# A fused streaming-encoder trunk on one core: the first pair of retention heads in halves of the features, its loads reordered, and two units of the conditioning vector made on TensorE

## The chip, the cores and the metric

The kernel runs on one core of a Trainium2 chip. The metric is the device time of one execution in microseconds (us), as the median of several runs. TensorE does the matmuls, VectorE (DVE in the rows) and ScalarE (ACT) the element-wise work, GpSimd (POOL) the rotary embedding and masks, and the SyncE queue (SP) issues nearly all transfers from HBM.

## The reference

The trunk has two layers. Each layer modulates a normed input with a conditioning vector, mixes over tokens, and then applies a channel mixer. The first mixer is retention with 8 heads, the second a stick-breaking attention; the first channel mixer is a dense SwiGLU, the second a top-2-of-8 expert SwiGLU. The input is 256 tokens of 1024 features, all in float32. What bears on this change is the beginning of the first layer:

```python
cond = jax.nn.silu(c)                                  # 1024 numbers
mod = cond @ ada_w[i] + ada_b[i]                       # ada_w[i]: 1024 x 6144
sh_m, sc_m, g_m, sh_f, sc_f, g_f = jnp.split(mod, 6, axis=-1)
h = modulate(rms_norm(x, norm_mix[i]), sh_m, sc_m)     # h * (1 + scale) + shift
y = retention(h, ...)                                  # starts with proj = h @ w_in, 1024 x 6144
q, k = rope(q), rope(k)
x = x + g_m[:, None, :] * y
```

## The kernel before

**Weights.** Every weight is fetched in chunks of 1 MB (a tile of 512 columns has two chunks, one for features 0 to 511 and one for 512 to 1023) into a ring of six raw buffers. ScalarE rounds a chunk into `w_hi` (L1079, two instructions of 128x1024), VectorE subtracts to get `w_lo` (L1449, two instructions), in a ring of three. TensorE then makes each product in three passes, `hi*hi`, `hi*lo`, `lo*hi` (L500, L501, L502, function `passes`). In the first layer the 256 tokens are two blocks, so a chunk is 24 matmuls of 128x512. Chunks 0 and 1 are queries and keys of the first two heads, 2 and 3 their values, 4 and 5 their gates; chunks 6 to 11 are those of the second pair of heads, and so on.

**The conditioning vector.** `cond @ ada_w` is made in units of 512 columns. For a unit VectorE adds eight slices of the weights, each times one column of `cond`, into `acc` (`ada_steps`: one L1465, seven L1468). TensorE transposes `acc` with four matmuls (`reduce_ada`, L539), and VectorE adds up the result and the bias (`mod_out`, L1487 and L1489). A unit's weights are two loads of 1 MB into the two halves of `ada` (`load_ada`, L285); each half is issued when the same half of the unit before has been read. Units 0 and 1 are the shift of the first layer, unit 2 the first half of its scale. The second half of the scale is not made so but with columns of `cond` as the moving operand: 32 float32 matmuls (64 passes, L573) from a tile of weights that is put into raw buffers 4 and 5 (`ada_first`).

**The start, in the order of each engine.**

- SP: unit 0, `x`, positions and frequencies, `ada_first`, unit 1, chunk 0, unit 2, chunks 1, 2, 3; then a wait until the columns have been read, and chunks 4 and 5.
- TensorE: transposes of unit 0, of the normed `x` (`transpose_x`, L546, eight matmuls per block of tokens), the 64 passes of the columns, transposes of units 1 and 2; then chunks 0 and 1 by blocks of tokens.
- VectorE: unit 0, the rotary angles (L1543 to L1559), the two normed blocks (L1500), units 1 and 2, `scol` (1 + scale times the gain of the norm), and per block `modulate` (L1510) and the split of `hT_lo` (L1515). ScalarE does the other half of the features (L1111) and `hT_hi` (L1118).

**The first pair and the loop.** Per pair of heads TensorE multiplies the tile of queries and keys, then that of values, waits for the rotary embedding (`roped`, six GpSimd instructions L463 to L470, which start when ScalarE has copied the queries and keys out with L1161), transposes them (L659), multiplies the gates, and makes the scores (L672, L673). The scores are masked on VectorE (`decayed`, L1596) and multiplied with the values (`mix`, L631 to L633) after the next pair's queries and keys. VectorE weaves the splits of weights with the steps of two units per pair (`woven`); the first pair makes units 3 and 4. The remaining three pairs are one loop, whose PE order is:

```python
pe.wait_ge(qk_ev, i)
pe.wait_ge(mod_ok, 2 * i + 1)
tile(0, m, (0, 1))
pe.wait_ge(mod_ok, 2 * i + 2)
mix(i - 1)
pe.wait_ge(qk_ev, i + 1)
reduce_ada(4, 0, m - 1)
```

Semaphores order all of this; nothing is planned at run time. An engine works in the order of its own program, so an instruction that waits holds up all behind it.

Of the kernel before, what the change touches and what calls it, by code (L numbers as in the profile page):

```python
# [16 lines left out]
P = 128  # L17
# [34 lines left out]
def trunk(nc, x_d, c_d, pos_d, ada_w, ada_b, norm_mix, norm_ff, ret_w_in, ret_gn, ret_w_out, kv_ada_w,  # L52
# [7 lines left out]
    with ctx:  # L60
# [68 lines left out]
        ada_first = raw[:, 4:6, :]  # L129
# [67 lines left out]
        small_in = sem("small_in"); pos_in = sem("pos_in"); x_in = sem("x_in"); rw_in = sem("rw_in")  # L197
# [6 lines left out]
        ada_step = sem("ada_step"); first_done = sem("first_done"); first_ok = sem("first_ok"); first_in = sem("first_in")  # L204
# [40 lines left out]
        def _(sp):  # L245
# [33 lines left out]
            def load_ada(u, h, k=0):  # L279

                t = u if u < 3 else u + 1
                w, t0 = (ada_w[0], 0) if t < 12 else (kv_ada_w, 12) if t < 16 else (ada_w[1], 16)
                if u > 0:
                    sp.wait_ge(ada_step, 8 * (u - 1) + 4 * (h + 1) + 16 * k)
                sp.dma_start(ada[:, h, :].rearrange("p (t n) -> p t n", t=4),  # L285
                             cols_of(w, h * 4 * P, k * 2 * TW + (t - t0) * TW, TW)).then_inc(ada_in[h], 16)


            for row, src in ((0, ada_b[0]), (48, kv_ada_b), (64, ada_b[1])):
                n = src.shape[0] // P  # L290
                sp.dma_start(rows[row:row + n, 0, :], src.rearrange("(r c) -> r c", c=P)).then_inc(small_in, 16)
            load_ada(0, 0)
            load_ada(0, 1)
            sp.dma_start(x[:, :, :], x_d[0].rearrange("(b p) d -> p b d", p=P)).then_inc(x_in, 16)
# [10 lines left out]
            for h in range(2):  # L305
                sp.dma_start(ada_first[:, h, :].rearrange("p (t n) -> p t n", t=4),
                             cols_of(ada_w[0], h * 4 * P, 3 * TW, TW)).then_inc(first_in, 16)
            load_ada(1, 0)
            load_ada(1, 1)
            load_half2(0, 0, w_r, 0, 0, K0)  # L310
            load_ada(2, 0)
            load_ada(2, 1)
            load_half2(1, 0, w_r, 4 * P, 0, K0)
            load_tile(2, 0, w_r, 0, V0)
            sp.wait_ge(first_done, 1)
            load_tile(4, 0, w_r, 0, G0)
            with sp.Fori(0, PAIRS - 1) as k:
                load_half2(6, k, w_r, 0, k * 2 * DK + 2 * DK, k * 2 * DK + (2 * DK + K0))
                load_ada(3, 0, k)
                load_half2(7, k, w_r, 4 * P, k * 2 * DK + 2 * DK, k * 2 * DK + (2 * DK + K0))  # L320
                load_ada(3, 1, k)
# [5 lines left out]
                load_ada(4, 0, k)  # L327
                load_half(10, k, w_r, 0, k * 2 * DV + (G0 + 2 * DV))
                load_ada(4, 1, k)
                load_half(11, k, w_r, 4 * P, k * 2 * DV + (G0 + 2 * DV))  # L330

            for m in range(8):
# [4 lines left out]
                if m in (0, 1):  # L337
                    load_ada(9, m)
                if m in (3, 4):
                    load_ada(10, m - 3)  # L340
                if m >= 6:
                    load_ada(11, m - 6)
# [7 lines left out]
            load_ada(12, 0)  # L350
            load_in(c + 2, 0, 1, 0)
            load_ada(12, 1)
            load_in(c + 3, 0, 1, 1)
            load_rows(c + 4, 0, ff_w_out[0], 0)
            load_ada(13, 0)
            load_in(c + 5, 0, 2, 0)
            load_ada(13, 1)
# [3 lines left out]
            load_ada(14, 0)  # L361
            load_in(c + 9, 0, 3, 1)
            load_ada(14, 1)
            load_rows(c + 10, 0, ff_w_out[0], 4 * P)
            with sp.Fori(0, 3) as k:
                for o in range(2):
                    load_in(c + 11 + 3 * o, k, 2 * k + (4 + o), 0)
                    load_in(c + 12 + 3 * o, k, 2 * k + (4 + o), 1)
                    load_ada(15 + o, 0, k)
                    load_rows(c + 13 + 3 * o, k, ff_w_out[0], k * 4 * P + (3 + o) * 2 * P)  # L370
                    load_ada(15 + o, 1, k)
            load_in(c + 29, 0, 10, 0)
            load_in(c + 30, 0, 10, 1)
            load_ada(21, 0)
            load_rows(c + 31, 0, ff_w_out[0], 9 * 2 * P)
            load_ada(21, 1)
# [6 lines left out]
            ada_after = {0: (22, 0), 1: (22, 1), 3: (23, 0), 4: (23, 1), 6: (24, 0), 8: (24, 1), 10: (25, 0), 11: (25, 1),  # L383
                         13: (26, 0), 14: (26, 1)}
# [47 lines left out]
        def _(pool):  # L432
# [47 lines left out]
            diagonal(0, diag0, MIX0 + G, 5)  # L480
            diagonal(1, diag1, FF0 + G, 11)
# [3 lines left out]
            for c in range(KC):  # L485
# [3 lines left out]
                if c == 5:  # L489
                    pool.wait_ge(ada_step, 27 * 8)  # L490
                    diagonal(2, diag2, MIX1 + G, 21)
            pool.wait_ge(gbc_done, 3)
            diagonal(3, diag3, FF1 + G, 27)
# [3 lines left out]
        def _(pe):  # L497
# [44 lines left out]
            def transpose_x(n, b):  # L542

                pe.wait_ge(xn_ok, NB * n + b + 1)
                for c in range(KC):
                    last = pe.transpose(ps[:, 2 * b + c // 4, (c % 4) * P:(c % 4 + 1) * P],  # L546
                                        (xn0 if n == 0 else xn)[:, b, c * P:(c + 1) * P], ident[:, :])
# [16 lines left out]
            reduce_ada(0, 6)  # L564
            transpose_x(0, 0)
            transpose_x(0, 1)

            pe.wait_ge(cond_ok, 1)
            pe.wait_ge(first_in, 32)
            for c in range(4):  # L570
                for kc in range(KC):
                    cols = slice(kc % 4 * TW + c * P, kc % 4 * TW + (c + 1) * P)
                    last = pe.matmul(ps[:, 5, c:c + 1], ada_first[:, kc // 4, cols], cond[:, kc:kc + 1],  # L573
                                     start=kc == 0, stop=kc == KC - 1)
            last.then_inc(first_done, 1)
            reduce_ada(1, 7)
            pe.wait_ge(mod_ok, 1)
            reduce_ada(2, 6)

# [39 lines left out]
            def tile_by_blocks(c, banks, q):  # L619

                for b, bank in enumerate(banks):
                    for h in range(2):
                        block_half(c, h, b, bank, q)
# [12 lines left out]
            def pair_of_heads(i, m):  # L636

                later = not isinstance(i, int)
                if later:
                    pe.wait_ge(qk_ev, i)  # L640
                    pe.wait_ge(mod_ok, 2 * i + 1)
                if later:
                    tile(0, m, (0, 1))
                else:
                    tile_by_blocks(0, (0, 1), 0)
                if later:
                    pe.wait_ge(mod_ok, 2 * i + 2)
                    mix(i - 1)
                    pe.wait_ge(qk_ev, i + 1)
                    reduce_ada(4, 0, m - 1)  # L650
                    pe.wait_ge(gs_ok, i)
                tile(2, m, (2, 3))
                if later:
                    transpose_r(i - 1)
# [10 lines left out]
                reduce_ada(3, 4, m)  # L665
                if later:
                    pe.wait_ge(r32_ok, i)
                else:
                    pe.wait_ge(mod_ok, 3)

                for hd in range(2):
                    pe.matmul(ps[:, 6 + hd, 0:S], qkT[:, 2 + hd, 0:P], qkT[:, hd, :], start=True, stop=True)  # L672
                    last = pe.matmul(ps[:, 6 + hd, S:384], qkT[:, 2 + hd, P:S], qkT[:, hd, P:S], start=True, stop=True)  # L673
                last.then_inc(sc_done, 1)

            pair_of_heads(0, 0)
# [6 lines left out]
            for m in range(5):  # L683
# [3 lines left out]
                if m == 1:  # L687
                    pe.wait_ge(mod_ok, 2 * PAIRS + 2)
                    mix(PAIRS - 1)
                    reduce_ada(10, 6)  # L690
                if m == 3:
                    pe.wait_ge(mod_ok, 11)
# [7 lines left out]
            reduce_ada(11, 4)  # L700
# [4 lines left out]
            reduce_ada(12, 5)  # L705
# [32 lines left out]
            def ff_two(i, m):  # L738

                for o in range(2):  # L740
                    c = U_FF + 2 + 3 * o
                    ff_in(c, m, 2 * i + (1 + o))
                    pe.wait_ge(mod_ok, 2 * i + (13 + o))
                    reduce_ada(13 + o, 3, i)
# [9 lines left out]
            pe.wait_ge(mod_ok, 23)  # L754
            reduce_ada(23, 3)
# [3 lines left out]
            pe.wait_ge(mod_ok, 24)  # L759
# [51 lines left out]
            def reduce_last(u):  # L811

                pe.wait_ge(ada_step, 8 * (u + 1))
                bank = (2, 2, 3)[u - 24]
# [4 lines left out]
            def scores(c):  # L819

                pe.wait_ge(kq_ev, 2 + 2 * (c // 4))
                if c == 1:
                    pe.wait_ge(mod_ok, 25)
# [48 lines left out]
            reduce_last(24)  # L872
# [46 lines left out]
            pe.wait_ge(gbc_ev, 3)  # L919
            reduce_last(25)  # L920
            reduce_last(26)
# [145 lines left out]
        def _(act):  # L1067
# [36 lines left out]
            def modulate(q, n, b, shift, hT_free, dst=hT_hi):  # L1104

                act.wait_ge(xT_done, 4 * n + 2 * b + 1)
                act.wait_ge(scol_ok, q + 1)
# [6 lines left out]
                for i in range(2):  # L1114
                    act.wait_ge(h32b_ok if i else h32a_ok, NB * q + b + 1)
# [19 lines left out]
            act.wait_ge(x_in, 16)  # L1135
            root_table()
            for b in range(NB):
                root_mean_square(0, b)
            act.wait_ge(ang_ok, 1)
            act.activation(sin[:, :, :], red, ACT.Sin).then_inc(rt_ok, 1)  # L1140
            act.activation(cos[:, :, :], tmp_r, ACT.Sin).then_inc(rt_ok, 1)
            split(0)
            split(1)
            split(2)
# [908 lines left out]
```

## Time and profile before

| | |
|---|---|
| median of 3 runs | 1625.49 us (1624.29 to 1627.39) |
| the profiled execution | 1626.12 us, of which the span of the core is 1624.4 us |
| TensorE busy with matmuls | 1549.2 us, 95% of the span |
| VectorE, ScalarE, GpSimd busy | 88%, 67%, 4% of the span |
| moved from and to HBM | 500.91 MB, mean 308 GB/s |
| mean granted clock of TensorE | 0.979 |

Times in the rows are us from the start of the span, unless ns is said. "Busy" of TensorE counts overlapping matmuls once, and a matmul's own duration is longer than the distance to the next one, since they are pipelined. "PEclk" is the share of TensorE's full clock that was granted: 1.00 is 2.4 GHz and 0.50 is 1.2 GHz.

### The profile page before, as it was taken

What the parts mean: (1) busy time and instruction counts of PE and PEld (TensorE: products, weight loads), DVE (VectorE), ACT (ScalarE), POOL (GpSimd) and SP (SyncE); (2) the same over time, 40 slices, a digit from 0 to 9 for tenths busy, and PEclk for the clock granted to TensorE, in tenths of its full rate; (3) what the DMA queues carried; (4) which work ended last, traced back from release to release, by engine and by line L of the source; (5) the groups of instructions that cost most, each with busy time, mean ns of one, the idle gap of its engine ahead of it and who ended that gap; (6) DMA issues with size and microseconds to landing.
All of it is one profiled execution on the core that took longest, in us unless ns stands there. A gap on an engine that the chain in (4) does not pass through costs nothing.

```text
span 1624.4 us, 22887 instructions
## 1 busy us (share of the span) xinstructions
PE 1549.2 (95%) x7310; PEld 1285.2 (79%) x7310; DVE 1422.0 (88%) x1604; ACT 1085.6 (67%) x1224; POOL 58.9 (4%) x47
## 2 busy tenths in 40 slices
PE   4899998999989998999999999999999999999996
PEld 4788876888869776888888888888888888888884
DVE  6989999788878766989989989989989989989995
ACT  3544445344366646878878878878878778778773
POOL 0212200000000110000000000000000000000000
PEclk8899999999999998999999999999999999999998
DMA  9977777788855424999999999999999999999991
GB/s 329 340 259 268 268 262 248 273 299 296 324 187 207 156 79 146 390 370 346 361 379 339 367 373 338 374 375 332 368 377 333 365 380 335 366 381 334 363 380 69
DMA packets 235114, 500.91 MB, mean 308 GB/s; under 512 B 9744, under 2 KB 40640, under 8 KB 235072
## 3 DMA queue, kind: packets, MB, share of 16 engines
q1 hardware_dynamic: 233904, 500.29, 84.8%
q8 instruction: 25, 0.41, 0.1%
q10 hardware_dynamic: 1168, 0.07, 0.1%
q14 instruction: 17, 0.14, 0.0%
HBM read 499.28 MB, written 1.05 MB: 308 GB/s over the span
## 4 chain that ended last, share of the span: by engine, by line
PE 81%; DVE 9%; DMA 4%; issue 3%; ACT 2%; POOL 1%; SPq 0%; DVEq 0%; ACTq 0%; POOLq 0%
PE ps L500 24%; PE ps L502 24%; PE ps L501 24%; DVE acc L1468 3%; DMA ada<-in_ada_w 2%; DVE w_lo L1449 2%; PE ps L981 2%; PE ps L772 1%; PE ps L774 1%; PE ps L776 1%; DMA raw<-in_ret_w_in 1%; DMA ada<-in_kv_ada_w 1%; PE ps L990 1%; PE ps L1014 1%; PE ps L991 0%
## 5 line engine op out<-in xcount | busy, mean ns | idle before, releaser
L1449 DVE TENSOR_TENSOR w_lo<-raw,w_hi 128x1024 fp32r<-128x1024 f32 x834 | 991.0, 1228 | 68.8 <-ACT w_hi L1079 56.6
L1079 ACT ACTIVATE w_hi<-raw 128x1024 fp32r<-128x1024 f32 x834 | 861.3, 1057 | 215.5 <-PE ps L502 189.1
L500 PE MATMUL ps<-w_hi,RA 128*128 128x512 f32 x1528 | 606.4, 397 | 11.4 <-DVE RA L1909 3.7
L502 PE MATMUL ps<-w_hi,RA 128*128 128x512 f32 x1528 | 597.1, 391 | 0.0
L501 PE MATMUL ps<-w_lo,RA 128*128 128x512 f32 x1528 | 596.5, 390 | 0.0
L500 PEld LDWEIGHTS ps<-w_hi,RA 128*128 128x128 f32 x1528 | 287.8, 188 | 70.8 <-issue 4.6
L502 PEld LDWEIGHTS ps<-w_hi,RA 128*128 128x128 f32 x1528 | 287.6, 188 | 61.2
L501 PEld LDWEIGHTS ps<-w_lo,RA 128*128 128x128 f32 x1528 | 288.1, 189 | 58.1 <-issue 0.7
L500 PE MATMUL ps<-w_hi,hT_hi 128*128 128x512 f32 x400 | 161.7, 404 | 10.2 <-DVE hT_lo L1515 6.2
L501 PE MATMUL ps<-w_lo,hT_hi 128*128 128x512 f32 x400 | 158.2, 395 | 0.0
L502 PE MATMUL ps<-w_hi,hT_lo 128*128 128x512 f32 x400 | 158.1, 395 | 0.0
L1468 DVE SCALAR_TENSOR_TENSOR acc<-ada,cond,acc 128x512 f32<-128x512 f32 x189 | 151.6, 802 | 3.1
L500 PEld LDWEIGHTS ps<-w_hi,hT_hi 128*128 128x128 f32 x400 | 76.8, 192 | 26.9 <-DVE hT_lo L1515 7.1
L502 PEld LDWEIGHTS ps<-w_hi,hT_lo 128*128 128x128 f32 x400 | 76.6, 191 | 16.8
L501 PEld LDWEIGHTS ps<-w_lo,hT_hi 128*128 128x128 f32 x400 | 76.9, 192 | 15.3
L1364 ACT ACTIVATE RA<-ps 128x512 fp32r<-128x512 f32 x56 | 33.4, 597 | 56.4 <-PE ps L981 56.4
L1898 DVE TENSOR_TENSOR RA<-ps,RA 128x512 fp32r<-128x512 f32 x56 | 38.5, 688 | 22.0 <-ACT RA L1364 19.2
L1465 DVE TENSOR_SCALAR acc<-ada,cond 128x512 f32<-128x512 f32 x27 | 13.1, 484 | 35.1 <-DMA ada<-in_ada_w 33.0
L1360 ACT ACTIVATE FA<-ps 128x512 f32<-128x512 f32 x56 | 33.4, 596 | 13.7 <-PE ps L502 13.7
L1894 DVE TENSOR_TENSOR FA<-ps,FA 128x512 f32<-128x512 f32 x56 | 38.3, 685 | 3.1 <-PE ps L502 3.1
L1214 ACT ACTIVATE FA<-ps 128x512 f32<-128x512 f32 x11 | 6.6, 598 | 44.6 <-PE ps L502 44.6
L981 PE MATMUL ps<-ident,FA 128*128 128x128 f32 x224 | 33.5, 272 | 0.9 <-DVE FA L1894 0.9
(247 smaller groups left out, 1017.1 us busy)
## 6 DMA issues: line engine op xcount, KB each, us to landing
raw<-in_moe_w_in SPq DMA_DIRECT2D x224, 1024.0 KB
raw<-in_moe_w_out SPq DMA_DIRECT2D x112, 1024.0 KB
ada<-in_ada_w SPq DMA_DIRECT2D x46, 1024.0 KB, 7.4
raw<-in_ff_w_in SPq DMA_DIRECT2D x44, 512.0 KB
raw<-in_ret_w_in SPq DMA_DIRECT2D x16, 1024.0 KB
raw<-in_ff_w_out SPq DMA_DIRECT2D x11, 1024.0 KB
raw<-in_ret_w_in SPq DMA_DIRECT2D x16, 512.0 KB
raw<-in_ret_w_out SPq DMA_DIRECT2D x8, 1024.0 KB
```

The lines of the kernel that those rows point to most:

```text
L500: pe.matmul(out, a_hi, b_hi, start=first, stop=False)
L501: pe.matmul(out, a_hi, b_lo, start=False, stop=False)
L502: return pe.matmul(out, a_lo, b_hi, start=False, stop=last)
L772: pe.matmul(o, w_hi[:, s, wc], a_hi[:, kc, :], start=kc == 0 and k % 2 == 0, stop=False, skip_group_check=True)
L981: last = pe.transpose(ps[:, 2, c * P:(c + 1) * P], e_g[:, c * P:(c + 1) * P], ident[:, :])
L1079: act.activation(w_hi[:, cn % RING, cols], raw[:, cn % RAW, cols], ACT.Copy).then_inc(hi_done, 1)
L1360: act.activation(e_sa, ps[:, 0, :], ACT.Silu).then_inc(esa_ok, 1)
L1364: act.activation(eT_hi.rearrange("p c s -> p (c s)"), ps[:, 2, :], ACT.Copy).then_inc(eTh_ok, 1)
L1449: v.tensor_tensor(w_lo[:, cn % RING, cols], raw[:, cn % RAW, cols], w_hi[:, cn % RING, cols].bitcast(f32), ALU.subtract).then_inc(lo_done, 1)
L1468: ins = v.scalar_tensor_tensor(a, ada[:, h, cols], cond[:, kc:kc + 1], a, ALU.mult, ALU.add)
L1894: v.tensor_tensor(e_g, ps[:, 1, :], e_sa, ALU.mult).then_inc(eg_ok, 1)
L1898: v.tensor_tensor(eT_lo.rearrange("p c s -> p (c s)"), ps[:, 2, :], eT_hi.rearrange("p c s -> p (c s)").bitcast(f32), ALU.subtract).then_i ...
```

## The change

The first pair of heads is no longer made tile by tile but in halves of the features. TensorE makes the products with features 0 to 511 for queries and keys, values and gates (new chunks 0, 1, 2), and then those with features 512 to 1023 (new chunks 3, 4, 5). So chunk 0 needs only the first halves of shift and scale. Both halves of the scale are now made with columns of `cond` on TensorE (`first_columns(0)` and `first_columns(1)`, 64 passes each), and the vector units go down from 27 to 26: units 0 and 1 are the shift, and units 2 and 3 (before 3 and 4) belong to the first pair. Normed and transposed features 512 to 1023 are copied out of PSUM as they are, and are modulated later, in place.

The order of loads becomes: unit 0, first columns, `x` in two blocks, positions, chunks 0 and 1, unit 1, chunk 2, second columns, chunk 3, a wait for the first columns, chunks 4 and 5. The angles move behind the split of chunk 1. The first pair has its own programs, which are not woven as in the loop. Everything from the second pair on keeps its order; only the numbers of the units are one lower.

```diff
 SP
             load_ada(0, 0)
             load_ada(0, 1)
-            sp.dma_start(x[:, :, :], x_d[0].rearrange("(b p) d -> p b d", p=P)).then_inc(x_in, 16)
+            load_first(0)
+            for b in range(NB):
+                sp.dma_start(x[:, b, :], x_d[0, b * P:(b + 1) * P, :]).then_inc(x_in[b], 16)
...
+            load_half2(0, 0, w_r, 0, 0, K0)
+            load_half(1, 0, w_r, 0, V0)
             load_ada(1, 0)
             load_ada(1, 1)
-            load_half2(0, 0, w_r, 0, 0, K0)
-            load_ada(2, 0)
-            load_ada(2, 1)
-            load_half2(1, 0, w_r, 4 * P, 0, K0)
-            load_tile(2, 0, w_r, 0, V0)
+            load_half(2, 0, w_r, 0, G0)
+            load_first(1)
+            load_half2(3, 0, w_r, 4 * P, 0, K0)
             sp.wait_ge(first_done, 1)
-            load_tile(4, 0, w_r, 0, G0)
+            load_half(4, 0, w_r, 4 * P, V0)
+            load_half(5, 0, w_r, 4 * P, G0)
...
                 load_half(8, k, w_r, 0, k * 2 * DV + (V0 + 2 * DV))
-                sp.wait_ge(ada_step, 26 + 16 * k)
+                sp.wait_ge(ada_step, 18 + 16 * k)
                 load_decay(k)
 TensorE
+            reduce_ada(0, 4)
+            first_columns(0)
             transpose_x(0, 0)
             transpose_x(0, 1)
...
+            def first_pair():
+                first_tile(0, 0, (6, 7))
+                pe.wait_ge(xT_ev, 4)
+                first_tile(1, 0, (0, 1))
+                pe.wait_ge(mod_ok, 1)
+                reduce_ada(1, 4)
+                pe.wait_ge(first_ok, 1)
+                first_columns(1)
+                first_tile(2, 0, (2, 3))
+                first_tile(3, 1, (6, 7))
+                first_tile(4, 1, (0, 1))
+                first_tile(5, 1, (2, 3))
+                pe.wait_ge(roped, 1)
...
+                last.then_inc(qkT_done, 1)
+                pe.wait_ge(qkT_ev, 1)
+                pe.wait_ge(v_ev, 1)
+                scores_of_pair()
+                reduce_ada(2, 4)
 ScalarE
+            first_modulate(0, 0)
+            split(0)
+            first_modulate(0, 1)
...
+            split(1)
+            split(2)
+            first_modulate(1, 0)
+            first_modulate(1, 1)
+            split(3)
             act.wait_ge(ang_ok, 1)
...
+                split(4)
+                act.wait_ge(rt_ok, 2)
+                act.wait_ge(w_used, before_half(4))
+                act.activation(qk, ps[:, 6:8, :], ACT.Copy).then_inc(qk_ev, 1)
+                split(5)
+                act.wait_ge(w_used, before_half(5))
+                act.activation(v_t, ps[:, 0:2, :], ACT.Copy).then_inc(v_ev, 1)
+                split(6)
+                act.wait_ge(w_used, before_half(6))
+                act.activation(gs, ps[:, 2:4, :], ACT.Silu).then_inc(gs_ok, 1)
+                act.wait_ge(qkT_done, 1)
+                act.activation(qkT.rearrange("p (n c) s -> p n (c s)", n=2), ps[:, 4:6, :], ACT.Copy)\
+                   .then_inc(qkT_ev, 1)
+                split(7)
 VectorE
+            mod_out(0, 4)
+            first_scale(0)
+            first_modulate(0, 0)
+            split(0)
+            first_modulate(0, 1)
...
+            split(1)
+            angles()
             ada_steps(1, 0, 8)
-            mod_out(0, 6)
-            ada_steps(2, 0, 8)
...
+            split(2)
+            mod_out(1, 4)
+            first_scale(1)
+            first_modulate(1, 0)
+            first_modulate(1, 1)
+            split(3)
+            split(4)
+            split(5)
+            woven(6, 0, (0, 4), 2, (0, 8))
+            ada_steps(3, 0, 8)
+            mod_out(2, 4)
```

`first_modulate(h, b)` modulates half `h` of the features of block `b` with two instructions of 128x128 on ScalarE and two on VectorE, and splits it with one of 128x512 on each. `first_tile(c, h, banks)` is 24 matmuls of chunk `c`, twelve per block. `first_scale(h)` is two small additions on VectorE after `first_columns(h)`.

## Rows read from the trace of the kernel before

**Rows 1.** Waits of TensorE in the stretch 84 to 250 us: us in total, times, longest.
```profile
PE ps L500 <- ACT FA L1182: 2.2, 1, 2.2
PE ps L500 <- DVE w_lo L1449: 0.6, 1, 0.6
```

**Rows 2.** Stretches: us, then PE, PEld, DVE, ACT, POOL busy, PEclk, DMA share, GB/s.
```profile
24.00:26.00 2.00, 2.00 (x18) 2.00 (x18) 1.82 (x4) 0.00 (x0) 0.00 (x0) 0.91 1.07 354
26.00:28.00 2.00, 2.00 (x11) 2.00 (x11) 1.93 (x3) 0.00 (x0) 0.00 (x0) 0.50 1.00 305
48.00:50.00 2.00, 2.00 (x7) 1.51 (x7) 1.90 (x5) 0.63 (x1) 0.00 (x0) 0.62 1.10 350
700.00:1600.00 900.00, 898.29 (x4096) 743.58 (x4094) 832.81 (x803) 717.76 (x781) 0.00 (x0) 1.00 0.97 356
```

**Rows 3.** Timeline, 9 to 38 us: start, duration, engine, line, what, idle before.
```profile
9.69 5.54 DVE L1468 SCALAR_TENSOR_TENSOR acc<-ada,cond,acc 128x512 f32<-128x512 f32 x7
15.15 0.16 DVE L1543 CAST stat<-pos_i 128x2 f32<-128x2 int32 x1
15.29 1.11 PE L539 MATMUL ps<-ident,acc 128*128 128x128 f32 x4 [6.78 <-DVE acc L1468]
17.89 0.23 DVE L1559 TENSOR_SCALAR FA<-FA 128x128 f32<-128x128 f32 x1
19.03 3.50 PE L546 MATMUL ps<-ident,FA 128*128 128x128 f32 x16 [2.63 <-DVE FA L1500]
22.36 10.67 PE L573 MATMUL ps<-cond,raw 128*128 128x1 f32 x64
22.84 0.49 DVE L1465 TENSOR_SCALAR acc<-ada,cond 128x512 f32<-128x512 f32 x1 [3.01 <-DMA ada<-in_ada_w]
37.06 2.00 ACT L1079 ACTIVATE w_hi<-raw 128x1024 fp32r<-128x1024 f32 x2 [6.68 <-DMA raw<-in_ret_w_in]
```

**Rows 4.** The passes of the columns (L573) in two stretches: count, ns min/median/max, first and last start.
```profile
L573 PE MATMUL ps<-cond,raw x10: 169/250/250, 22.4 to 23.3; 128*128 128x1 f32 x10
L573 PE MATMUL ps<-cond,raw x20: 352/352/352, 26.3 to 30.3; 128*128 128x1 f32 x20
```

**Rows 5.** Timeline, 39 to 48 us.
```profile
39.55 2.35 DVE L1449 TENSOR_TENSOR w_lo<-raw,w_hi 128x1024 fp32r<-128x1024 f32 x2
41.68 1.49 ACT L1111 ACTIVATE FA<-ps,modc,scol 128x128 f32<-128x128 f32 x4
43.87 1.29 DVE L1515 TENSOR_TENSOR hT_lo<-FA,hT_hi 128x512 fp32r<-128x512 f32 x2 [0.69 <-ACT hT_hi L1118]
44.61 0.79 PE L500 MATMUL ps<-w_hi,hT_hi 128*128 128x512 f32 x1 [6.19 <-DVE hT_lo L1515]
46.06 0.63 PE L500 MATMUL ps<-w_hi,hT_hi 128*128 128x512 f32 x1
47.34 0.63 PE L500 MATMUL ps<-w_hi,hT_hi 128*128 128x512 f32 x1
```

**Rows 6.** Timeline of GpSimd: first and last of the six instructions of the first rotary embedding.
```profile
59.30 1.30 POOL L463 TENSOR_TENSOR FA<-FA,gate_m 128x512 f32<-128x512 f32 x1 [56.75 <-ACT FA L1161]
68.01 2.12 POOL L470 TENSOR_TENSOR FA<-FA 128x512 f32<-128x512 f32 x1
```

**Rows 7.** Timelines of TensorE and ScalarE: the copy of `qkT`, start of the second pair, `mix(0)`.
```profile
71.81 1.01 ACT L1176 ACTIVATE FA<-ps 128x1024 f32<-128x1024 f32 x1
83.70 0.48 PE L500 MATMUL ps<-w_hi,hT_hi 128*128 128x512 f32 x1
94.68 0.59 PE L631 MATMUL ps<-FA 128*128 128x256 f32 x2
```

**Rows 8.** Timeline of VectorE: the masked scores and the statistics of the first pair.
```profile
87.98 0.95 DVE L1596 TENSOR_TENSOR FA<-ps,FA 128x768 f32<-128x768 f32 x1
97.47 1.43 DVE L1603 BATCH_NORM_STATS2 stat<-ps 128x6 f32<-128x256 f32 x4 [2.36 <-PE ps L633]
```

**Rows 9.** All that touches `ada`, 30 to 250 us: us from a load's issue to its landing.
```profile
DMA to landing us min/median/max: 5.1/7.6/11.5
```

More of the change, by code:

```diff
@@ L563, in _, with first_columns @@
             pe.transpose(ps[:, 4, P:P + 48], rows[0:48, 1, :], ident[0:48, 0:48]).then_inc(vecT_done, 1)
-            reduce_ada(0, 6)
+            def first_columns(n):
+                for h in range(2):
+                    pe.wait_ge(first_in[2 * n + h], 16)
+                    for t in range(4):
+                        for c in range(4):
+                            last = pe.matmul(ps[:, 5, c:c + 1], ada_first[n][:, h, t * TW + c * P:t * TW + (c + 1) * P],
+                                             cond[:, 4 * h + t:4 * h + t + 1], start=h == 0 and t == 0 and c == 0,
+                                             stop=h == 1 and t == 3, skip_group_check=True)
+                last.then_inc(first_done, 1)
+            pe.wait_ge(cond_ok, 1)
+            pe.wait_ge(vec_ok, 1)
+            reduce_ada(0, 4)
+            first_columns(0)
             transpose_x(0, 0)
             transpose_x(0, 1)
[L568 to L578, printed above, removed]
             def transpose_r(i):
@@ L636, in pair_of_heads @@
             def pair_of_heads(i, m):
[L638 to L651, printed above, removed]
+                pe.wait_ge(qk_ev, i)
+                pe.wait_ge(mod_ok, 2 * i)
+                tile(0, m, (0, 1))
+                pe.wait_ge(mod_ok, 2 * i + 1)
+                mix(i - 1)
+                pe.wait_ge(qk_ev, i + 1)
+                reduce_ada(3, 0, m - 1)
+                pe.wait_ge(gs_ok, i)
                 tile(2, m, (2, 3))
-                if later:
-                    transpose_r(i - 1)
+                transpose_r(i - 1)
                 pe.wait_ge(roped, i + 1)
@@ L664, in pair_of_heads @@
                 pe.wait_ge(qkT_ev, i + 1)
[L665 to L676, printed above, removed]
+                reduce_ada(2, 4, m)
+                pe.wait_ge(r32_ok, i)
+                scores_of_pair()
+            first_pair()
             with pe.Fori(0, PAIRS - 1) as k:
@@ L1153, in pair_of_heads @@
             def pair_of_heads(i, m):
-                later = not isinstance(i, int)
-                if later:
-                    split(2, m)
+                split(2, m)
                 split(3, m)
-                if later:
-                    act.wait_ge(roped, i)
+                act.wait_ge(roped, i)
                 act.wait_ge(w_used, before_half(2, m))
@@ L1574, in _ @@
-            split(1)
-            modulate(0, 0, 1, MIX0 + SH)
-            split(2)
+            mod_out(0, 4)
[3 more added lines that the diff above has]
+            first_modulate(0, 1)
+            for b in range(NB):
+                dve.wait_ge(xT_done, 2 * b + 2)
+                v.tensor_copy(h32_0[:, b, 6:8, :].rearrange("p c q -> p (c q)"),
+                              ps[:, 2 * b + 1, S:2 * S]).then_inc(xT_ev, 1)
+            split(1)
+            angles()
```

330 lines of the change are left out of this document (185 added, 145 removed).

## The prediction

> **What bounds the kernel now.** I read the stretches first. In the long expert stage TensorE is busy 898.29 of 900 us at full clock [rows 2]. I then looked at who waits from the start of the second pair of heads to 250 us: TensorE stands still for 2.8 us there in all [rows 1]. Later waits of TensorE hang on its own results, not on absolute time. So the time is set by the moment at which TensorE gets through the start, and a shift of that moment reaches the end undiminished. My marks are the first matmul of the second pair, at 83.70 us, and `mix(0)`, at 94.68 us [rows 7]. Between them lie 48 matmuls of 128x512, so a chunk of 24 costs 5.5 us at the upper clock. This also says what is worth nothing: VectorE loses a whole unit (6.0 us, one L1465 and seven L1468 [rows 3]), but it isn't what TensorE waits for after the start.
>
> The start itself is a timeline. TensorE begins chunk 0 at 44.61 us [rows 5], after a wait for `hT_lo`; units 1 and 2 had waited for their loads [rows 3]. It begins at the lower clock level: three matmuls take 1.28 us, 0.43 each [rows 5], and the granted clock only rises in the stretch 48 to 50, whose mean of 0.62 puts the rise near 49.5 [rows 2].
>
> **The change, in order of time.** I follow the new programs with these durations.
>
> *First columns, to chunk 0.* They now come before the transposes of `x`, right behind those of unit 0, which are issued from 15.29 to about 16.2 us [rows 3]. A pass costs 0.11 us at the upper clock level (10 starts in 0.9 to 1.0 us) and 0.21 at the lower (20 starts in 4.0 us) [rows 4]; 64 passes are 7.1 or 13.5 us. Before, they had sixteen transposes of `x` right ahead of them; now only four. I take the lower level: 29.7 us. Eight transposes of block 0 at 0.22 [rows 3] bring 31.5. Modulating and splitting took 2.9 us from ScalarE's first instruction to the first matmul [rows 5]; with two instead of four instructions of 0.37 per engine it is 2.2, so `hT` is there at 33.9. The weights have landed by then (the sixth MB at 22.84 [rows 3]), but `split(0)` stands behind this modulation on both engines: ScalarE's first quarter ends at 34.2 and VectorE's 1.2 us later. TensorE starts chunk 0 at **35.5**, 9.1 us earlier than now. If the columns ran at the upper level, 29.1.
>
> *Chunks 0 and 1, unit 1.* Chunk 0 starts at the lower level as now and takes 7.2 us (to 42.7), chunk 1 ends at 48.2. Then TensorE must reduce unit 1. VectorE has by then: the splits of chunk 0 to 36.6; block 1 modulated, 38.7; two copies out of PSUM, 39.4; the splits of chunk 1, 42.2, as ScalarE too does them only after its copies; the angles, 3.0 us [rows 3], 45.2; unit 1, 6.1 us, **51.3**. The loads of unit 1 (eighth and ninth MB) are there since about 31, at 2.8 us per MB (five MB between the landings at 22.84 and 37.06 [rows 3]). TensorE stands still for 3.1 us; its wait took the place of that for the loads.
>
> *Second columns.* Reducing unit 1 ends at 51.8. The second 64 passes now stand in the middle of the matmuls, with chunk 2 queued behind them, and nothing covers them. Their price is between 7.1 us and 13.5; I take the 10.67 that this form took in the profile [rows 3], part of it at each level: 62.5.
>
> The granted clock fell from 1.00 to 0.50 in the stretches 24 to 28, while exactly these passes kept TensorE busy for every us of them [rows 2], and it rose only under wide matmuls. So chunk 2 starts at the lower level, pays again what chunk 0 pays now (4.9 us at 0.43 instead of 0.23 per matmul: 2.3 us), takes 7.8 us and ends at 70.3. The Trainium skill ("TensorE: Matmul & The Clock Gate", Part 1, What's actually happening) says that activity releases the throttle, and that the gate follows how busy the engine has been. By that rule the passes would hold the upper level: the second rival. The profile's rows speak against it.
>
> *Second half of the features.* VectorE has waited for the columns since about 54. From 62.5: the small additions 0.6, two blocks at 2.1, so 67.3; chunk 3 is split right after, with ScalarE ahead by one quarter: 69.0 and 70.2. Chunks 3, 4, 5 then run on end to end to 86.7. The rotary embedding starts with the copy after chunk 3 (75.8 + 1.1) and took 10.8 us beside a busy VectorE (59.30 to 70.13 [rows 6]): 87.7, so a wait of 1.0. Transposes 0.9; the copy of `qkT`, 1.0 us [rows 7], on which TensorE now waits with nothing to do (before, the gates' tile lay over it): **89.8**.
>
> *Unit 2.* This is the new wait that I think matters most. The last instruction of TensorE's first pair is the reduction of unit 2, and it needs all eight steps. VectorE weaves them with the splits of chunks 6 and 7; ScalarE rounds chunk 7 only after the copy of `qkT`. Behind 89.8 come in series: ScalarE's quarter 1.05, a VectorE quarter 1.2, two steps 1.5, a quarter 1.2, two steps 1.5: **96.2**. The scores cover 1.3 us of it; TensorE idles about 5. The second pair starts at 96.7 instead of 83.7: +13.0.
>
> *Unit 3 and the loads behind it.* The second half of unit 3's weights may only be issued when unit 2 is complete, at 96.2. `decayed(0)` stands behind the first step of unit 4 (its place in the loop is unchanged; now it happens at 87.98 [rows 8]). On SP's queue, in front of unit 4's load, are: unit 3's half, chunk 11, and both parts of chunk 12; all are issued only after 96.2. The shortest time from issue to landing of an `ada` load is 5.1 us [rows 9]; three more MB at 2.8 make 13.5: 109.7. One step 0.5 and `decayed` 0.95 [rows 8]: `mix(0)` at **111.2** instead of 94.68, **+16.5**. What these loads cost beyond the +13.0 is thus 3.5; it is nothing if they land by 106, and 6 with the median of 7.6 us. VectorE had 2.4 us to spare at `mix(0)` [rows 8], and all engines start on the next stage from that wait, so I add nothing behind it.
>
> **The sum.** -9.1 (start of chunk 0) up to the mark becomes +13.0 by: wait for unit 1 3.1, its reduction 0.5, second columns 10.7, chunk 2 at the lower level 2.3; wait for unit 2 and its reduction about 5.5; the rest, 0.0, is the transposes and the copy of `qkT`, now bare, against the same work and the reduction of unit 3 before. Then +3.5 by the loads. The profiled execution took 1626.1 us, 0.6 more than the median, so 1626.1 + 16.5 - 0.6 = **1642.0**.
>
> **The rivals.**
>
> - *The clock holds through the second columns.* They take 7.1 us and chunk 2 5.5; VectorE's half of the features then comes 1 us late for chunk 3. Gain against the forecast 4.9: +11.6, 1637. For it: the engine comes from two chunks of wide matmuls. Against: the 3 us wait, and the fall in [rows 2]. 0.18.
> - *The late chain is short.* Clock as above, and unit 4's weights come in time, or the first columns run at the upper level: +5 to +8, 1631 to 1634. 0.11.
> - *TensorE alone.* VectorE is never late: 35.5 + 7.2 + 5.5 + 0.5 + 7.1 + 21.8 (four chunks) + 0.9 + 1.1 + 1.3 + 0.5 = 81.4 at the first mark, 2.3 before now: 1623, no measurable change. 0.07.
> - *Faster.* The earlier start is kept. The mechanism is the pace of the first columns: at the upper level everything after them moves 6.4 us forward, chunk 0 to 29.1, and with VectorE in time the mark is at 75.0: -8.7, 1617. It decides once VectorE completes unit 1 before TensorE ends chunk 1 and unit 2 before the scores. For it: the loads do allow it, and VectorE has a unit less. Against: the row of programs above, in which each is late by 3 to 5 us. 0.10.
> - *Worse.* Columns at 13.5 us (+2.8), or loads at the median or more of [rows 9] (+2.5 and up), a further fall of the clock in the new waits: +19 to +24, 1645 to 1650. 0.07.
>
> **How the numbers follow.** The forecast has 0.47, with a range of its own from 1639 to 1645. All times within 0.2% (3.3 us) of 1625.5 count as no change; that is about what a measurement of this kernel can tell. So faster 0.10, same 0.07, slower 0.83. The range 1628 to 1647 leaves out the two lowest cases (0.17) and half of the worst one.
>
> **What would show it.** First L500 near 35.5 us; the second passes near 52 to 62 with a granted clock of 0.5 in their later part; TensorE's wait before the reduction of unit 1 about 3 us, and before that of unit 2 about 5, both on L1468; the second pair near 97 and the first L631 near 111, behind L1596 and a load of `ada`. The prediction is wrong if the second columns keep the clock, or if chunk 7's splits don't hold up unit 2, since with both gone the sum is near zero.

## The result and the profile after

| | before | changed |
|---|---|---|
| median | 1625.85 us (1624.29 to 1627.39, 4 runs) | 1656.88 us (1651.99 to 1661.06, 4 runs) |
| span of the profiled execution | 1624.4 us | 1651.1 us |

The ratio is 1.0187 (95% interval 1.0167 to 1.0208): slower by 31 us, where 16.5 were forecast. The changed kernel's times spread over 9 us; the profiled execution (1652.81 us) is one of its shorter ones, so the trace shows 26.7 of the 31 us.

The timeline of the changed kernel, with the rows that answer to [rows 3, 5, 6, 7, 8]. L546 is `reduce_ada`, L581 the columns, L507 the first pass, L1518 the `w_lo` split, L684 `mix`, L1696 `decayed`:

```profile
16.12 13.65 PE L581 MATMUL ps<-cond,raw 128*128 128x1 f32 x64
35.43 0.76 PE L507 MATMUL ps<-w_hi,hT_hi 128*128 128x512 f32 x1 [2.15 <-DVE w_lo L1518]
50.67 0.63 PE L546 MATMUL ps<-ident,acc 128*128 128x128 f32 x4 [2.43 <-DVE acc L1537]
51.14 1.06 PE L581 MATMUL ps<-cond,FA 128*128 128x1 f32 x9
...
77.13 1.29 POOL L470 TENSOR_TENSOR FA<-FA,gate_m 128x512 f32<-128x512 f32 x1 [74.58 <-ACT FA L1214]
86.59 1.32 POOL L477 TENSOR_TENSOR FA<-FA 128x512 f32<-128x512 f32 x1
...
96.41 0.66 PE L546 MATMUL ps<-ident,acc 128*128 128x128 f32 x4 [3.31 <-DVE acc L1537]
96.82 0.67 PE L507 MATMUL ps<-w_hi,hT_hi 128*128 128x512 f32 x1
112.91 0.62 DVE L1534 TENSOR_SCALAR acc<-ada,cond 128x512 f32<-128x512 f32 x1 [3.28 <-DMA ada<-in_ada_w]
113.45 0.94 DVE L1696 TENSOR_TENSOR FA<-ps,FA 128x768 f32<-128x768 f32 x1
114.49 1.19 PE L684 MATMUL ps<-FA 128*128 128x256 f32 x2 [4.88 <-issue]
```

The reader sees the predicted stations: chunk 0 at 35.43 (35.5 forecast), the wait for unit 1 (2.4 us, forecast 3.1), the wait for unit 2 (3.3 us, forecast 5), the second pair at 96.82 (96.7). `mix(0)` is at 114.49 where 111.2 was forecast, behind a load of `ada` and L1696, as written.

The granted clock in the second columns and in the third pair (columns as in [rows 2]):

```profile
50.00:52.00 2.00, 1.33 (x13) 1.36 (x13) 2.00 (x3) 0.00 (x0) 0.00 (x0) 1.00 1.03 397
52.00:54.00 2.00, 2.00 (x14) 2.00 (x14) 1.56 (x3) 0.00 (x0) 0.00 (x0) 0.65 1.08 366
60.00:62.00 2.00, 2.00 (x11) 2.00 (x11) 0.00 (x0) 0.00 (x0) 0.00 (x0) 0.50 0.26 95
170.00:180.00 10.00, 7.14 (x27) 6.38 (x28) 9.71 (x19) 4.75 (x6) 0.00 (x0) 0.66 0.40 137
```

In each row PEclk is the third number from the end. The clock fell under passes that kept TensorE busy without a gap, as in [rows 2]. Here a wait of 2.4 us lay before them; a run below has none and shows the same fall.

In the list of TensorE's waits from 115 to 300 us, two entries have no counterpart in the kernel before, where the same list was read from 84 to 300 us:

```profile
PE ps L684 <- issue: 5.1, 2, 4.9
...
PE ps L598 <- DVE FA L1723: 3.0, 1, 3.0
```

The first is `mix(0)`. The second is `transpose_r(1)` (the transposes of the first pair's normed result) at 172.86 us, waiting for VectorE's group norm; the clock's 0.66 in the last stretch above lies around it. So I compared the first L684 (before: L631) of the four pairs, which is where the delay can be seen to grow:

| start of | before | changed | delay |
|---|---|---|---|
| second pair | 83.7 | 96.8 | 13.1 |
| `mix(0)` | 94.7 | 114.5 | 19.8 |
| `mix(1)` | 134.0 | 155.7 | 21.7 |
| `mix(2)` | 173.2 | 201.1 | 27.9 |
| `mix(3)` | 215.0 | 242.5 | 27.5 |
| end of span | 1624.4 | 1651.1 | 26.7 |

The four traces of variants of the kernel before have `mix(0)` between 93.2 and 93.9 us, so a single delay is known to about 1 us. From `mix(2)` on nothing is added. Of the 26.7 us the forecast had the first row, half of the step to the second, and nothing of the 7 to 8 us behind it.

### The profile page after: what moved, and what is told of

The parts are those of the page before. It is cut to its first block, busy times and chain, and to the rows that moved or that the text cites. A ratio compares the mean times of both kernels' runs of the same rounds, so it can differ in the third digit from the quotient of the medians.

```text
span 1651.1 us, 23012 instructions
## 1 busy us (share of the span) xinstructions
PE 1573.2 (95%) x7370; PEld 1306.0 (79%) x7370; DVE 1420.0 (86%) x1598; ACT 1085.5 (66%) x1226; POOL 62.0 (4%) x47
## 4 chain that ended last, share of the span: by engine, by line
PE 80%; DVE 11%; issue 3%; ACT 2%; DMA 2%; DVEq 0%; ACTq 0%; SPq 0%
PE ps L507 23%; PE ps L509 23%; PE ps L508 23%; DVE acc L1537 3%; DVE w_lo L1518 3%; DMA ada<-in_ada_w 2%; PE ps L581 2%; PE ps L1020 1%; PE ps L811 1%; PE ps L813 1%; PE ps L815 1%; PE ps L1029 1%; PE ps L1053 0%; PE ps L1030 0%; PE ps L1054 0%
## 5 line engine op out<-in xcount | busy, mean ns | idle before, releaser
L1518 DVE TENSOR_TENSOR w_lo<-raw,w_hi 128x1024 fp32r<-128x1024 f32 x834 | 995.7, 1233 | 72.4 <-ACT w_hi L1118 60.0
L507 PE MATMUL ps<-w_hi,RA 128*128 128x512 f32 x1528 | 606.7, 397 | 11.1 <-DVE RA L2006 3.7
L507 PEld LDWEIGHTS ps<-w_hi,RA 128*128 128x128 f32 x1528 | 288.0, 188 | 70.6 <-issue 5.0
L507 PE MATMUL ps<-w_hi,hT_hi 128*128 128x512 f32 x400 | 163.3, 408 | 5.6 <-issue 3.5
L1537 DVE SCALAR_TENSOR_TENSOR acc<-ada,cond,acc 128x512 f32<-128x512 f32 x182 | 145.8, 801 | 5.3 <-DMA ada<-in_ada_w 2.4
L507 PEld LDWEIGHTS ps<-w_hi,hT_hi 128*128 128x128 f32 x400 | 77.8, 195 | 22.9 <-issue 6.5
L1534 DVE TENSOR_SCALAR acc<-ada,cond 128x512 f32<-128x512 f32 x26 | 13.7, 528 | 33.2 <-DMA ada<-in_ada_w 32.3
```

Source lines behind the costliest of these rows:

```text
L507: pe.matmul(out, a_hi, b_hi, start=first, stop=False)
L1518: v.tensor_tensor(w_lo[:, cn % RING, cols], raw[:, cn % RAW, cols], w_hi[:, cn % RING, cols].bitcast(f32), ALU.subtract).then_inc(lo_done, 1)
L1537: ins = v.scalar_tensor_tensor(a, ada[:, h, cols], cond[:, kc:kc + 1], a, ALU.mult, ALU.add)
```

## The experiments

Times are medians of four or more runs, the ratio is to the kernel before in the same batch. Its median was 1628.0 us in one batch (the cut embedding, units 2 and 3, the columns before chunk 1, the six fills) and 1625.3 to 1625.9 in the others; a comparison of two kernels from different batches is therefore uncertain by 3 us or so. Edits are to the changed kernel, if nothing else is said.

**The changed kernel again.**

> The changed kernel once more, unaltered. Its four times so far fall into two groups, near 1652 and near 1661 us. If VectorE's debt decides whether one more wait of TensorE (with a fall of the clock behind it) appears in a later pair, both groups come again, and a trace of the slower group shows an idle stretch of TensorE that the faster one lacks. If the groups came from something outside the kernel, one value comes.

1656.64 us (1653.7 to 1659.94), ratio 1.0194 (1.0167 to 1.0221). The spread is there again, without two clear groups. No trace is of an execution near 1661 us, so the spread stays unexplained.

**The wait for the decay table.** In the changed kernel SyncE issues no load for 35 us: it stands before the first decay table, waiting for two steps of unit 2. In the timeline of SyncE:

```profile
52.97 0.40 SPq L266 DMA_DIRECT2D raw<-in_ret_w_in  x1
88.64 0.35 SPq L312 DMA_DIRECT2D FA<-in_decay_table  x1
89.23 0.40 SPq L266 DMA_DIRECT2D raw<-in_ret_w_in  x1
91.22 0.37 SPq L286 DMA_DIRECT2D ada<-in_ada_w  x1
```

```diff
-                sp.wait_ge(ada_step, 18 + 16 * k)
+                sp.wait_ge(*((first_done, 2) if isinstance(k, int) else (ada_step, 18 + 16 * k)))
```

The first turn of the loop of loads is taken out of it (`k` is then a plain number), so only that turn waits for the second columns instead.

> SyncE waits for the second columns instead of for two steps of unit 2 before it loads the first decay table, so the table and chunk 9 land before 88 us instead of after. Theory L (a burst of loads behind that wait makes mix(0) late): about 1.4 MB less in the burst, 3 to 4 us less at mix(0) (from 114.5 to about 111), and 3 to 8 us less in all. Theory D (TensorE's and VectorE's own work sets mix(0)): mix(0) within 1 us of 114.5 and the total within 2 us of the changed kernel's.

1657.40 us, ratio 1.0195 (1.0170 to 1.0221). `mix(0)` came at 112.1 instead of 115.2 in the trace of the kernel beside it, as theory L said; `mix(1)` at 154.7 instead of 156.7, `mix(3)` at 243.5, as without the edit. The wait behind which the loads pile up does make `mix(0)` late, but taking it away is worth nothing at the end: the loop gives the 3 us back.

**Chunk 7 rounded early.**

```diff
                 split(6)
+                split(7)
                 act.wait_ge(w_used, before_half(6))
...
-                split(7)
```

> ScalarE rounds chunk 7 ahead of the gates and of the copy of qkT. Step of the prediction under test: unit 2 is late because chunk 7's splits stand behind that copy. If so, the reduction of unit 2 is ready some 3 to 4 us earlier (from 96.4 to about 93) and the total falls by 3 to 8 us. Rival: VectorE is late by its own work under the rotary embedding (83 to 90 us); then the reduction moves by 1 us or less and so does the total.

1654.15 us, ratio 1.0177 (1.0151 to 1.0203). The reduction of unit 2 was issued at 96.36 us, against 96.50 without the edit: the rival. ScalarE now had chunk 7 rounded at 86.2 us, and VectorE still worked without a gap from 83.4 to 96.3. It does the same without the edit, with its first instructions stretched by the rotary embedding (GpSimd's six instructions end at 87.9 us):

```profile
83.34 2.02 DVE L1518 TENSOR_TENSOR w_lo<-raw,w_hi 128x1024 fp32r<-128x1024 f32 x1 [1.60 <-ACT w_hi L1118]
85.28 1.51 DVE L1534 TENSOR_SCALAR acc<-ada,cond 128x512 f32<-128x512 f32 x1
86.83 1.63 DVE L1537 SCALAR_TENSOR_TENSOR acc<-ada,cond,acc 128x512 f32<-128x512 f32 x1
```

The prediction's chain over the copy of `qkT` was the right length by chance; VectorE's own work is as long. The 2.5 us of the median are within the spread.

**A quarter of the second columns.**

```diff
-                        for c in range(4):
+                        for c in range(1 if n else 4):
```

> Leaves out three quarters of the second columns (16 of 64 passes; 384 features of the scale then have another value). If the 64 passes cost their own time and keep the clock down, TensorE gets to chunk 2 about 9 us earlier (from 61.5 to about 53) and loses less at the lower clock: the second pair starts 8 to 12 us earlier and the total falls by 8 to 14 us. Rival: VectorE and the loads set the second pair's start anyway; then less than 4 us comes out at the end.

1644.94 us, ratio 1.0127 (1.0096 to 1.0158). The second pair starts at 87.25 us instead of 97.27, so three quarters of the passes and their share of the lower clock cost 10.0 us there, and 11.7 at the end. This is the largest single cost found, and without it 20 us are still left.

**Units 2 and 3 narrow.** Steps two to eight of both units work on 8 columns.

> The changed kernel; seven of the eight steps of units 2 and 3 work on 8 columns only (the gate of the first layer then has another value). VectorE has about 10 us less to do before the loop, and unit 2 is complete some 4 us earlier. Theory V (VectorE's own work in series sets the second pair and mix(0), and its debt costs 7 us later): second pair 3 to 4 us earlier, mix(0) 4 to 7, total 8 to 13 us lower. Rival L (the burst of loads sets mix(0)): mix(0) moves by less than 3 us and the total by less than 4.

1651.14 us, ratio 1.0139 (1.0120 to 1.0157). Neither theory had it whole. The second pair started 2.1 us earlier (95.13), `mix(0)` at 115.0 as before: there VectorE idled for loads.

```profile
99.28 0.49 DVE L1536 TENSOR_SCALAR acc<-ada,cond 128x512 f32<-128x512 f32 x1 [4.97 <-DMA ada<-in_ada_w]
...
104.54 1.01 DVE L1539 SCALAR_TENSOR_TENSOR acc<-ada,cond,acc 128x8 f32<-128x8 f32 x4 [3.98 <-DMA ada<-in_ada_w]
...
112.98 1.02 DVE L1536 TENSOR_SCALAR acc<-ada,cond 128x512 f32<-128x512 f32 x1 [5.34 <-DMA ada<-in_ada_w]
```

So `mix(0)` is set by the loads behind unit 2, and not by VectorE's own work. The median is 5.5 us lower, but the trace does not show where: it is of the longest of the four executions (1653.34 us), is about 6 us ahead at `mix(2)` (195.5), about 1 at `mix(3)` (241.9) and not at all at the end. That gain stays open.

**The second columns before chunk 1.**

```diff
+                pe.wait_ge(first_ok, 1)
+                first_columns(1)
                 pe.wait_ge(xT_ev, 4)
                 first_tile(1, 0, (0, 1))
                 pe.wait_ge(mod_ok, 1)
                 reduce_ada(1, 4)
-                pe.wait_ge(first_ok, 1)
-                first_columns(1)
```

> The changed kernel with the second columns right after chunk 0 instead of after the reduction of unit 1, so that TensorE does them while VectorE makes unit 1. Prediction's step under test: the 2 to 3 us wait for unit 1 is a cost of its own. Then chunk 3 starts 2 to 4 us earlier and so does the second pair; of that, the total shows all (2 to 4 us less) if TensorE's start passes through, and nothing if VectorE and the loads set the pace of the loop.

1651.64 us, ratio 1.0147 (1.0129 to 1.0165). The wait for unit 1 is gone, the second pair starts at 95.05 us, 2.2 earlier, and the total is 5 us lower, more than the 2 to 4 expected. This run also answers whether the wait ahead of the columns makes the clock fall. Here wide matmuls lead straight up to the passes, with TensorE busy all the time, and it falls all the same (the passes, then two stretches with columns as in [rows 2]):

```profile
42.57 9.74 PE L581 MATMUL ps<-cond,FA 128*128 128x1 f32 x64
44.00:46.00 2.00, 2.00 (x20) 2.00 (x19) 1.90 (x5) 0.00 (x0) 0.00 (x0) 1.00 1.06 382
48.00:50.00 2.00, 2.00 (x11) 2.00 (x11) 1.89 (x4) 0.00 (x0) 0.00 (x0) 0.50 0.96 273
```

**The rotary embedding cut.** In the loop, GpSimd's six instructions work on a sixteenth of their elements:

```diff
+                if not isinstance(i, int):
+                    t1, t2, o1, o2, ta, tb, cs, sn = (t[:, :, :, 0:4] for t in (t1, t2, o1, o2, ta, tb, cs, sn))
```

> The changed kernel; the rotary embedding of the second to fourth pair works on 4 of every 64 features only (the others keep what the buffer held), so GpSimd hardly touches SBUF there. In the changed kernel mix(1) and mix(2) come 41.2 and 45.4 us after the mix before them; in the kernel before 39.3 both times. Theory C (VectorE is late, so the rotary embedding falls on its splits and steps, which it slows to double): the distances return to 39 to 40 and the total falls by 6 to 9 us. Rival D (loads and waits carry the delay): distances stay above 41 and the total falls by less than 3.

1645.69 us (1641.21 to 1646.05), ratio 1.0100 (1.0077 to 1.0123). `mix(0)` is no earlier, but the mixes are now 39.3 us apart, as theory C said; the total falls by 11 us (14 to 15 by the ratios), more than its 6 to 9. The first matmuls of the four mixes (here L686, one row each):

```profile
L686 PE MATMUL ps<-FA x4: 379/379/454, 115.6 to 117.2; 128*128 128x256 f32 x4
L686 PE MATMUL ps<-FA x4: 377/378/379, 155.0 to 156.5; 128*128 128x256 f32 x4
L686 PE MATMUL ps<-FA x4: 377/378/379, 194.2 to 195.7; 128*128 128x256 f32 x4
L686 PE MATMUL ps<-FA x4: 377/378/379, 233.5 to 235.0; 128*128 128x256 f32 x4
```

**The kernel before, with a debt of VectorE, with and without the embedding.** Fills of 128x1024 between VectorE's first pair and its loop:

```diff
             pair_of_heads(0, 0)
+            for _ in range(6):
+                steps.link(v.memset(gate_f[:, :], 0.0))
```

> The kernel before, with six fills of 128x1024 in the unused gate buffer on VectorE between the first pair and the loop: 4 to 7 us of work that nothing needs. If VectorE's slack behind mix(0) absorbs it, as the prediction took it, the total rises by 0 to 3 us. If a debt of VectorE is passed on and grows in the loop, mix(0) to mix(2) drift apart and the total rises by 5 to 12 us.

> The kernel before with the rotary embedding of the second to fourth pair cut in the same way: the control for theory C. If the embedding costs only where VectorE is late, the total is within 2 us of the kernel before and the mixes stay 39.3 us apart. If GpSimd's share of SBUF costs in any case, it is 5 us or more faster.

> The kernel before with the six fills on VectorE and with the cut rotary embedding in the second to fourth pair. Theory C (the lag costs because the embedding then lies on VectorE's splits and steps): mixes 39 to 40.5 us apart, total within 4 us of 1621.7, the cut embedding without the fills. Rival (VectorE is the bound as soon as it is late): total 7 us or more above 1621.7, as the fills cost without the cut.

> The kernel before with two fills instead of six, some 2.3 us of VectorE's time instead of 7.1. If VectorE's spare time of 2.4 us at mix(0) absorbs a small lag, the total stays within 1.5 us of the kernel before; if any lag grows, it rises by 3 us or more.

| kernel before, with | full embedding | cut embedding |
|---|---|---|
| no fills | 1625.8 | 1621.71, ratio 0.9972 (0.9962 to 0.9982) |
| two fills (2.3 us) | 1625.31, ratio 0.9998 (0.9988 to 1.0007) | |
| six fills (7.1 us) | 1635.46, ratio 1.0049 (1.0031 to 1.0068) | 1621.94, ratio 0.9980 (0.9967 to 0.9992) |

Seven us of debt cost about 8, and nothing at all when the embedding is cut. The expectation for the cut alone was missed: it makes the kernel before 4 us faster, so the embedding costs something there too. That leaves about 7 of the 11 us that the cut takes off the changed kernel (10 by the ratios) as the price of the change. In the trace with the debt, `mix(0)` is where it was (93.9 us); then come 135.4, 179.6 and 223.3, so the delay appears only behind it. The clearest measure is the time from `mix(0)` to `mix(3)`, from the traces:

| from `mix(0)` to `mix(3)`, us | full embedding | cut embedding |
|---|---|---|
| kernel before | 120.3 | 117.8 |
| kernel before, two fills | 122.1 | |
| kernel before, six fills | 129.4 | 117.8 |
| changed kernel | 128.1 (again: 128.4) | 117.9 |

With the embedding cut, all three kernels take the same time here. So the 7.7 us that the changed kernel loses in this stretch come only together with the embedding. The lead of VectorE goes with it: `decayed` ends 5.8 us before `mix(0)` begins in the kernel before, 5.2 with two fills (they mostly fill a wait of 1.9 us for a load), 0.6 with six, and 0.1 in the changed kernel. This is how the loss comes about. VectorE's row of the second pair in the kernel before, on time:

```profile
131.40 1.22 DVE L1449 TENSOR_TENSOR w_lo<-raw,w_hi 128x1024 fp32r<-128x1024 f32 x1
132.53 0.75 DVE L1468 SCALAR_TENSOR_TENSOR acc<-ada,cond,acc 128x512 f32<-128x512 f32 x1
133.20 1.22 DVE L1449 TENSOR_TENSOR w_lo<-raw,w_hi 128x1024 fp32r<-128x1024 f32 x1
134.33 0.75 DVE L1468 SCALAR_TENSOR_TENSOR acc<-ada,cond,acc 128x512 f32<-128x512 f32 x1
135.00 1.22 DVE L1449 TENSOR_TENSOR w_lo<-raw,w_hi 128x1024 fp32r<-128x1024 f32 x1
```

and the same instructions with the debt. The embedding starts where it did (135.78 us, 135.26 in the kernel before), but they have slid under it:

```profile
135.25 1.22 DVE L1449 TENSOR_TENSOR w_lo<-raw,w_hi 128x1024 fp32r<-128x1024 f32 x1
136.38 1.77 DVE L1468 SCALAR_TENSOR_TENSOR acc<-ada,cond,acc 128x512 f32<-128x512 f32 x1
138.07 2.30 DVE L1449 TENSOR_TENSOR w_lo<-raw,w_hi 128x1024 fp32r<-128x1024 f32 x1
140.30 1.78 DVE L1468 SCALAR_TENSOR_TENSOR acc<-ada,cond,acc 128x512 f32<-128x512 f32 x1
141.99 2.31 DVE L1449 TENSOR_TENSOR w_lo<-raw,w_hi 128x1024 fp32r<-128x1024 f32 x1
```

The changed kernel has the same picture in its second pair:

```profile
158.35 2.30 DVE L1518 TENSOR_TENSOR w_lo<-raw,w_hi 128x1024 fp32r<-128x1024 f32 x1
160.58 1.77 DVE L1537 SCALAR_TENSOR_TENSOR acc<-ada,cond,acc 128x512 f32<-128x512 f32 x1
162.27 2.31 DVE L1518 TENSOR_TENSOR w_lo<-raw,w_hi 128x1024 fp32r<-128x1024 f32 x1
164.50 3.48 DVE L1537 SCALAR_TENSOR_TENSOR acc<-ada,cond,acc 128x512 f32<-128x512 f32 x2
167.90 1.41 DVE L1703 BATCH_NORM_STATS2 stat<-ps 128x6 f32<-128x256 f32 x4
```

**The three moves together** (early decay wait, chunk 7 early, columns before chunk 1).

> The changed kernel with all three moves: the early wait for the first decay table, chunk 7 rounded early, the second columns before chunk 1. If the delays of the start are separate and the loop passes a lead on, the total is near 1645 (5 us for the columns' place, 3 for unit 2 and 3 for the loads). If VectorE's lag against TensorE sets the loop, the total stays within 3 us of 1651.6, that of the columns' move alone. Neither expects it below the kernel before.

> The same, and the rotary embedding of the second to fourth pair works on 4 of every 64 features only. Theory C: without GpSimd beside VectorE the distances between the mixes are 39 to 40 us, so the total is 6 to 10 us below that of the three moves alone, near 1639. Rival: the loads hold the loop up, and the distances stay above 41.

> The three moves with only 16 of the 64 second passes (384 features of the scale then have another value). This is what the order by halves would give if the second scale cost TensorE little. If the halves are a gain in themselves, TensorE reaches the second pair near 84 us, as before, and the total comes to 1630 or less. If VectorE's work in series is the limit all the same, the total stays above 1635.

1651.17 us (ratio 1.0156, 1.0139 to 1.0173), 1640.80 (1.0092, 1.0075 to 1.0108) and 1646.10 (1.0122, 1.0105 to 1.0139). All three moves give what the columns' move gives alone. With the cut embedding the three distances are 41.0, 39.3 and 39.3 us. With a quarter of the passes the second pair starts at 88.74 us, later than the 83.70 of the kernel before: TensorE waits 2.68 us for the splits of chunk 3 and 4.53 for unit 2. So the order by halves is no gain in itself here, even with a quarter of the columns. No variant of the changed kernel beats the kernel before.

## Why the prediction was right in sign and wrong in size

- **The start of chunk 0, the wait for unit 1, the second pair at 96.7: right**, each within 1 us. (Three terms don't follow exactly: 31.5 + 2.2 is 33.7 and not 33.9, 87.7 + 0.9 + 1.0 is 89.6 and not 89.8, and chunk 0 gets 7.2 us "as now", where the 24 matmuls took 7.9 in the kernel before. It did take 7.2, by luck: the clock rose 3.5 us after its start instead of 5.) So was the reason to expect a loss: serial work on three engines replaced by longer serial work.
- **The second columns: right in kind, sized a little low.** The 64 passes took 12.3 us of TensorE's busy time (10.7 in the sum; 10.3 to 12.7 in the six traces that have all of them in this place), since the clock fell after the first ones; the rival in which it holds did not happen. Chunk 2 made up for part of it with 6.9 us (7.8 in the sum). One reason given for the lower clock was misread: that it "rose only under wide matmuls". In the kernel before it rose at the end of the sixteen transposes of `x` (273 ns for the shortest, 421 for most); in the changed kernel the same sixteen all ran at the lower level (L546 is `transpose_x` in the kernel before, L557 in the changed one):

```profile
L546 PE MATMUL ps<-ident,FA x16: 273/421/472, 19.0 to 22.3; 128*128 128x128 f32 x16
L557 PE MATMUL ps<-ident,FA x16: 421/421/454, 29.6 to 32.9; 128*128 128x128 f32 x16
```

  The quarter of the passes puts the whole item, with chunk 2 at the lower clock, at 10.0 us for three quarters.
- **Unit 2 late by the copy of `qkT`: the place was right, the cause not.** Rounding chunk 7 earlier moved the reduction by 0.1 us. VectorE, in part slowed by the embedding, was as late. TensorE waited 3.3 us for it and not 5, since the scores, at a granted clock of 0.52, took 2.9 us (1.3 in the sum).
- **The loads behind unit 2: right, sized low.** The sum took the shortest issue-to-landing of 5.1 us; the second half of unit 3 took 7.9 (96.52 to 104.42). So unit 4's half landed at 112.9 instead of 109.7, which is nearly all of the 3.3 us between the forecast and `mix(0)`.
- **"I add nothing behind it": wrong, and the failed step.** The reason given was that VectorE had 2.4 us to spare at `mix(0)`, and that all engines leave that wait together. But VectorE leaves it later relative to TensorE than before: `decayed` ended 0.1 us before `mix(0)` began, while in the kernel before it was 5.8 us ahead of it [rows 7, 8]. The splits and steps that used to lie in that lead now come behind `mix(0)`. The statistics of the first pair, for which VectorE had waited 2.4 us, start 5 us after the last matmuls of `mix(0)`, which end at 118.8 us:

```profile
123.84 1.41 DVE L1703 BATCH_NORM_STATS2 stat<-ps 128x6 f32<-128x256 f32 x4
```

  The lag puts the embedding on VectorE's splits and steps, makes it later still, and ends in a 3.0 us wait of TensorE with a fall of the clock. The price is 7.7 us between `mix(0)` and `mix(3)`. The tables of debts show it apart from the change: 2.3 us of extra work are absorbed, 7.1 are not, and without the embedding neither the debt nor the change costs anything in this stretch.
- **The remaining 4 us** are the difference between the profiled execution and the median of a kernel whose runs spread by 9 us. That is open. Without the embedding the account closes better: cut in both, the changed kernel is 24 us slower by the medians (1645.69 against 1621.71) and 22 by the spans of the traces (1644.0 against 1621.8), and all 22 are there at `mix(0)` (115.6 against 93.2).

## What to carry to other kernels

Slack has to be measured as the lead of one engine over the other at the point where they meet, and a change that delays both can use it up though the wait itself is gone. Fills that nothing needs, as in the table of debts, measure that slack. A shorter way to the first matmul was worth nothing here, since the work behind it, on the other engines and on the queue, wasn't shortened too: print where each engine is when the steady loop begins, not when it starts to work. A lead gained at one mark (3 us at `mix(0)` by the earlier loads) has to be followed to the end of the next loop before it is counted.

## What the runs showed of the hardware

- An instruction of VectorE with two large operands in SBUF takes about twice as long beside GpSimd's (L1449 1.22 to 2.30 us, L1468 0.75 to 1.77), while those that read PSUM don't change: the statistics took 1.43 us for four beside GpSimd (L1603) and 1.41 without (L1703). The Trainium skill says this in "GPSIMD Engine Reference", Key points: the two share their SBUF interfaces, with contention for instructions with two SBUF inputs (and for those in a 2-port mode). The trace agrees. It also shows an instruction with one large operand in SBUF slowed even more, to three times; whether that one runs in a 2-port mode, no run here shows. The same L1534 took 0.48 us alone and 1.51 beside the embedding, and the scaling of the group norm, with and without it:

```profile
101.25 3.39 DVE L1623 TENSOR_SCALAR FA<-FA,stat 128x256 f32<-128x256 f32 x4
171.67 1.14 DVE L1723 TENSOR_SCALAR FA<-FA,stat 128x256 f32<-128x256 f32 x4
```

  What was not expected is how much hangs on where the two meet: 7 to 8 us of the whole kernel.
- Single-column float32 passes without a gap did not keep the upper clock: it fell at 52.6 us, and a pass went from 0.11 to 0.21 us; it fell also where wide matmuls stood right ahead of them. The rule of the Trainium skill that was weighed in the prediction ("TensorE: Matmul & The Clock Gate", Part 1, What's actually happening: that the gate follows how busy the engine has been) would have kept it. The traces speak against it.
